# Spreading PEER gates to a table per expert: one fp32 product per token, or two products in the rounded 32-bit form

## The chip, the cores and the metric

The kernel runs on one core of a Trainium2 chip. The metric is the device time of one execution in microseconds (us). Engines are named as in the profile: PE is TensorE's matmuls, PEld its weight loads, DVE VectorE, ACT ScalarE, POOL GpSimd, SP SyncE, which starts most transfers.

## What is computed

One block of a network on x (1024 tokens x 1024): a gated recurrence and an attention in parallel, an output projection, then PEER, a retrieval over 128 x 128 single-neuron experts, and a last norm. The change is in PEER:

```python
q = (hf @ w_q).reshape(t, 8, 2, 128)
sc = einsum('thpc,hpnc->thpn', q, subkeys)
s1, i1 = top_k(sc[:, :, 0], 16); s2, i2 = top_k(sc[:, :, 1], 16)
top_s, top_p = top_k(pairs of s1 + s2, 16)
e1, e2 = the two numbers (0..127) of each chosen expert     # 8 heads x 16 = 128 per token
gates = softmax(top_s).reshape(t, 128)
pre = einsum('td,tkd->tk', h, u_tab[e1 * 128 + e2])
y = einsum('tk,tkd->td', gelu(pre) * gates, v_tab[e1 * 128 + e2])
```

## The kernel before, in words

The first three tiles of 128 tokens ("row tiles") fetch the rows of their chosen experts one by one. The other five (640 tokens) are dense: `pre` is computed for all 16384 experts and multiplied by a table of gates that is zero where an expert wasn't chosen. This table, for each token a 128 x 128 matrix over first and second number, is what the change makes in another way.

`experts_up` does this stage. Its outer loop runs over 128 blocks c of 128 experts, each cut into four quarters q (512 in all), and every engine has its own list of work by quarter. In a block:

- SP loads the next 512 KB of the turned u table (`wq_then_u`, two buffers), and stores the block's activations.
- ACT rounds it (`high`, L1637, written as `wq_then_uT_hi`); DVE (or POOL for blocks below 42 and the last four) subtracts for the rest (`low`, L1804 or L1706).
- PE multiplies (L1603): 48 products of 320 columns per block, 24 for each half of the tokens, in the rounded 32-bit form (float32r), of which one product is one pass. ACT takes the gelu of each half (L1651).
- POOL fetches rows for the row tiles by indirect DMA (L1717) into a ring of seven, and DVE multiplies and sums them (`dot`, L1737), about four per block.
- From quarter 136 on, DVE turns the choices of a dense tile into numbers (`key`, seven steps, L1240, L1244, L1246, one step every four quarters, so over some seven blocks), PE transposes them and DVE keeps them (`keep`).
- From quarter 166 to 500, 160 groups g of four tokens are spread, about two per block. For group g, which PE spreads at quarter Q: DVE writes a one-hot of the first number at Q-5 (`hot_group`, L1814); ACT writes |n - second| at Q-5 (`distance`, L1661) and relu(gate - gate * |n - second|), that is the gate where n is the second number and else 0, at Q-4 (`gate`, L1669); PE multiplies the two, per token a 128 x 128 x 128 product in fp32 (`spread_out`, L1591), and ACT copies the group out at Q (L1644). SP stores eight groups at a time (2 MB).

An engine works its list in order, so a wait holds all that stands behind it. ACT's list of a quarter is: `high`, `gelu`, `spread_out`, `distance`, `gate`. DVE's is: `low`, `key`, `keep`, `hot_group`, dots. `high(c+1)` stands at the first quarter of block c and `low(c+1)` at the second, so both may lag about four quarters behind PE before PE waits. `experts_down` (L2098) follows; the change doesn't touch it.

Of the kernel before, what the change touches and what calls it, by code (L numbers as in the profile page):

```python
# [4 lines left out]
ALU = mybir.AluOpType  # L5
# [8 lines left out]
P = 128  # L14
# [1432 lines left out]
def experts_up(nc, d, m, sem):  # L1447
# [12 lines left out]
    GROUP, SLOTS, PART = 4, 4, 8  # L1460
    GROUPS = P // GROUP
# [36 lines left out]
    with ExitStack() as own_memory:  # L1498
# [5 lines left out]
        first_hot = sb("first_hot", [P, SLOTS, GROUP, NK])  # L1504
        second = sb("gated_second_hot", [P, SLOTS, GROUP, NK])
# [7 lines left out]
        minus = sb("minus_second_and_gate", [P, 2, 2, P])  # L1513
# [13 lines left out]
        hot_done, apart_done, gates_hot = sem("hot_done"), sem("second_apart"), sem("gates_hot")  # L1527
# [9 lines left out]
        each = lambda values: values.rearrange("p (t a) -> p t a", a=1).to_broadcast([P, GROUP, NK])  # L1537

# [7 lines left out]
        with nc.Block() as block:  # L1546
# [37 lines left out]
            def _(pe):  # L1584
                def spread_out(g):
                    pe.wait_ge(hot_done, g + 1)
                    pe.wait_ge(gates_hot, g + 1)
                    if g >= 2:
                        pe.wait_ge(spread_read, g - 1)
                    for j in range(GROUP):  # L1590
                        last = nc.tensor.matmul(spread_ps[:, g % 2, j], first_hot[:, g % SLOTS, j],  # L1591
                                                second[:, g % SLOTS, j], start=True, stop=True)
                    last.then_inc(spread_done, 1)
# [14 lines left out]
                def turn_route(t):  # L1608
                    pe.wait_ge(key_step, KEY_STEPS * (nth[t] + 1))
                    if dense_nth[t]:  # L1610
                        pe.wait_ge(routeT_done, 2 * dense_nth[t])
# [18 lines left out]
            def _(act):  # L1630
# [23 lines left out]
                def distance(g):  # L1654
                    i, first = g // GROUPS, g % GROUPS * GROUP
                    if first == 0:
                        act.wait_ge(routeT_done, 2 * i + 2)
                    if g >= SLOTS:
                        act.wait_ge(spread_done, g - SLOTS + 1)
                    for j in range(GROUP):  # L1660
                        last = A(second[:, g % SLOTS, j], m.iota[:], ACT.Abs,  # L1661
                                 bias=minus[:, i % 2, 0, first + j:first + j + 1])
                    last.then_inc(apart_done, 1)

                def gate(g):
                    i, first = g // GROUPS, g % GROUPS * GROUP
                    act.wait_ge(apart_done, g + 1)
                    for j in range(GROUP):
                        last = A(second[:, g % SLOTS, j], second[:, g % SLOTS, j], ACT.Relu,  # L1669
                                 scale=minus[:, i % 2, 1, first + j:first + j + 1],  # L1670
                                 bias=routeT[:, i % 2, 2, first + j:first + j + 1])
                    last.then_inc(gates_hot, 1)

                for q in range(QUARTERS):
# [15 lines left out]
                    for g in hots_at(q):  # L1690
                        distance(g)
# [36 lines left out]
            def _(dve):  # L1728
# [3 lines left out]
                v.tensor_copy(places[:], m.iota[:, 0:TOP])  # L1732

# [56 lines left out]
                def keep(t, n):  # L1790
                    i = dense_nth[t]
                    if n == 0:
# [3 lines left out]
                        v.tensor_copy(routeT[:, i % 2], route_ps[:]).then_inc(routeT_done, 1)  # L1796
                    else:
                        dve.wait_ge(routeT_done, 2 * i + 1)
                        v.tensor_scalar(minus[:, i % 2], routeT[:, i % 2, 1:3], -1.0, None, ALU.mult
                                        ).then_inc(routeT_done, 1)  # L1800
# [6 lines left out]
                def hot_group(g):  # L1807
                    i, first = g // GROUPS, g % GROUPS * GROUP
                    tokens = slice(first, first + GROUP)
                    if first == 0:  # L1810
                        dve.wait_ge(routeT_done, 2 * i + 1)
                    if g >= SLOTS:
                        dve.wait_ge(spread_done, g - SLOTS + 1)
                    v.tensor_tensor(first_hot[:, g % SLOTS], keys, each(routeT[:, i % 2, 0, tokens]), ALU.is_equal  # L1814
                                    ).then_inc(hot_done, 1)

                for q in range(KEYS_FROM, QUARTERS + 4):
# [8 lines left out]
                    for n in range(2):  # L1826
                        for t in tiles_at(q, TURN_AFTER + 2 + n):
# [474 lines left out]
```

## Time and profile before

| | |
|---|---|
| median of 3 runs | 2829.38 us (2820.77 to 2845.56) |
| profiled execution, its span | 2830.1 us |
| PE, PEld busy | 2707.8 us (96%), 2374.9 us (84%) |
| DVE, ACT, POOL busy | 2303.6 (81%), 1251.7 (44%), 1441.5 us (51%) |
| transfers | 762.66 MB, mean 269 GB/s over the span |
| gates are spread | 1151 to 1893 us |

A busy share is the union of an engine's instructions over the span. Ends of matmuls are modelled, so for PE the distance from one start to the next tells more than a duration. On ACT and DVE too an instruction begins before the recorded end of the one in front, so what it adds is the distance between starts. "Idle before, releaser" names what ended a wait.

### The profile page before, as it was taken

The page shows a single profiled execution, that of the slowest core. Times are in us where ns is not written, and L with a number is a line of the kernel's source. Part 1 is how long each engine was busy: PE and PEld are TensorE (multiplying, and loading weights), DVE is VectorE, ACT ScalarE, POOL GpSimd, SP SyncE. Part 2 cuts the span into 40 slices and gives each one's busy share as a digit, 9 for nine tenths or more (in the row PEclk, how much of TensorE's full clock was granted, in tenths as well). Part 3 has the DMA queues.
Part 4 walks back from the last instruction along what each step waited for, and adds up shares of the span by engine and source line. Part 5 has one row for each costly group of instructions (what it writes and reads, how often), then busy time and mean ns, then how long its engine had stood idle before and what let it go on. Part 6 is the DMA issues. An engine that isn't in the chain of part 4 may idle for free. (4 is left out here: it accounts for less than half of the span.)

```text
span 2830.1 us, 39999 instructions
## 1 busy us (share of the span) xinstructions
PE 2707.8 (96%) x14923; PEld 2374.9 (84%) x14923; DVE 2303.6 (81%) x4084; ACT 1251.7 (44%) x2540; POOL 1441.5 (51%) x932
## 2 busy tenths in 40 slices
PE   7999799989999999999999999989999999999998
PEld 6777566449999999999999999987778888878877
DVE  3293896238989999797989797776999999999997
ACT  4244443113332222798888888873222222222222
POOL 1011321004328885666767566662666656656562
PEclk9999899989999999999999999999999999999999
DMA  4110100223228886999999999999999999999995
GB/s 119 42 38 23 60 1 13 85 75 101 71 62 309 302 296 218 336 368 387 382 398 393 380 391 394 390 390 337 374 369 383 385 387 388 386 389 372 391 378 216
DMA packets 332114, 762.66 MB, mean 269 GB/s; under 512 B 23232, under 2 KB 158400, under 8 KB 329360
## 3 DMA queue, kind: packets, MB, share of 16 engines
q0 software_dynamic: 111104, 403.02, 37.9%
q1 hardware_dynamic: 220096, 353.67, 35.2%
q10 hardware_dynamic: 720, 3.41, 0.3%
q8 instruction: 118, 1.93, 0.3%
q14 instruction: 76, 0.62, 0.1%
HBM read 667.73 MB, written 92.27 MB: 269 GB/s over the span
## 5 line engine op out<-in xcount | busy, mean ns | idle before, releaser
L1968 POOL DMA_INDIRECT v_rows<-in_peer_v,row_numbers x336 | 525.0, 1562 | 347.6 <-DVE y_rest L2041 202.1
L1603 PE MATMUL expert_pre<-h2T,wq_then_uT_hi 128*128 128x320 f32 x4096 | 674.7, 314 | 22.7 <-ACT wq_then_uT_hi L1637 20.3
L1717 POOL DMA_INDIRECT u_rows<-in_peer_u,row_numbers x384 | 554.1, 1443 | 243.5 <-DVE row_weights L1737 154.7
L1603 PEld LDWEIGHTS expert_pre<-h2T,wq_then_uT_hi 128*128 128x128 f32 x4096 | 613.9, 190 | 25.0 <-issue 24.9
L2098 PE MATMUL expert_out<-v_hi,w_hi 128*128 128x512 f32 x1280 | 501.9, 392 | 17.7 <-DVE w_lo L2019 16.7
L1737 DVE CUSTOM_DVE_ANT_0 u_rows<-u_rows,h_rows_kept 128x1024 f32<-128x1024 f32 x384 | 491.9, 1310 | 23.7 <-DMA u_rows<-in_peer_u,row_numbers 23.5
L2098 PE MATMUL expert_out<-v_lo,w_hi 128*128 128x512 f32 x1280 | 500.1, 391 | 0.0
L2098 PE MATMUL expert_out<-v_hi,w_lo 128*128 128x512 f32 x1280 | 500.0, 391 | 0.0
L2041 DVE SCALAR_TENSOR_TENSOR y_rest<-v_rows,row_weights,y_rest 128x1024 f32<-128x1024 f32 x256 | 327.4, 1283 | 25.9 <-DMA v_rows<-in_peer_v,row_numbers 25.5
L1603 PE MATMUL expert_pre<-h2T,wq_then_uT_lo 128*128 128x320 f32 x2048 | 343.2, 310 | 0.2 <-POOL wq_then_uT_lo L1706 0.2
L1603 PEld LDWEIGHTS expert_pre<-h2T,wq_then_uT_lo 128*128 128x128 f32 x2048 | 311.8, 188 | 0.6 <-POOL wq_then_uT_lo L1706 0.5
L1988 ACT ACTIVATE w_hi<-pick_memory 128x640 fp32r<-128x640 f32 x128 | 94.7, 740 | 481.0 <-DVE pick_memory L2012 470.8
L2098 PEld LDWEIGHTS expert_out<-v_hi,w_hi 128*128 128x128 f32 x1280 | 241.6, 189 | 72.8 <-DVE w_lo L2019 21.2
L2098 PEld LDWEIGHTS expert_out<-v_hi,w_lo 128*128 128x128 f32 x1280 | 241.4, 189 | 50.4
L2098 PEld LDWEIGHTS expert_out<-v_lo,w_hi 128*128 128x128 f32 x1280 | 241.6, 189 | 49.6
L1669 ACT ACTIVATE gated_second_hot<-gated_second_hot,routeT,minus_second_and_gate 128x128 f32<-128x128 f32 x640 | 265.8, 503 | 0.2
L1986 ACT ACTIVATE v_hi<-pick_memory 128x1024 fp32r<-128x1024 f32 x128 | 134.8, 1053 | 161.0 <-PE expert_out L2098 80.1
L1661 ACT ACTIVATE gated_second_hot<-iota,minus_second_and_gate 128x128 f32<-128x128 f32 x640 | 205.9, 409 | 0.0
L1651 ACT ACTIVATE expert_acts<-expert_pre 128x320 f32<-128x320 f32 x256 | 111.5, 436 | 212.3 <-PE expert_pre L1603 180.9
L1637 ACT ACTIVATE wq_then_uT_hi<-wq_then_u 128x1024 fp32r<-128x1024 f32 x127 | 134.8, 1062 | 125.9 <-DMA wq_then_u<-in_peer_u_turned 124.2
L1309 POOL TENSOR_TENSOR wq_then_uT_lo<-wq_then_u,wq_then_uT_hi 128x1024 fp32r<-128x1024 f32 x30 | 72.4, 2412 | 223.2 <-ACT wq_then_uT_hi L1404 223.2
L1804 DVE TENSOR_TENSOR wq_then_uT_lo<-wq_then_u,wq_then_uT_hi 128x1024 fp32r<-128x1024 f32 x82 | 100.5, 1225 | 102.9 <-ACT wq_then_uT_hi L1637 93.4
(326 smaller groups left out, 4171.1 us busy)
## 6 DMA issues: line engine op xcount, KB each, us to landing
wq_then_u<-in_peer_u_turned SPq DMA_DIRECT2D x128, 512.0 KB
pick_memory<-in_peer_v SPq DMA_DIRECT2D x128, 512.0 KB
pick_memory<-acts_dram SPq DMA_DIRECT2D x128, 320.0 KB
acts_dram<-expert_acts SPq DMA_DIRECT2D x124, 320.0 KB
pick_memory<-gates_dram SPq DMA_DIRECT2D x31, 1280.0 KB
gates_dram<-pick_memory SPq DMA_DIRECT2D x19, 2048.0 KB
wq_then_u<-in_peer_wq SPq DMA_DIRECT2D x32, 512.0 KB, 3.9
w_in_columns<-in_w_in SPq DMA_DIRECT2D x20, 512.0 KB, 4.0
```

The source lines that it names most:

```text
L1603: last = nc.tensor.matmul(pre[:, (2 * c + half) % 4, 0:WIDTH], part[:, c % 2, k], m.h2T[:, t, k, HALVES[half]], start=n == 0, stop=n == le ...
L1637: A(uhi[:, c % 2], u[c % U_RING], ACT.Copy).then_inc(uhi_done, 1)
L1651: A(act_out[:, c % 2, half * WIDTH:(half + 1) * WIDTH], pre[:, (2 * c + half) % 4, 0:WIDTH], ACT.Gelu_apprx_tanh).then_inc(act_done, 1)
L1661: last = A(second[:, g % SLOTS, j], m.iota[:], ACT.Abs, bias=minus[:, i % 2, 0, first + j:first + j + 1])
L1669: last = A(second[:, g % SLOTS, j], second[:, g % SLOTS, j], ACT.Relu, scale=minus[:, i % 2, 1, first + j:first + j + 1], bias=routeT[:, i ...
L1717: pool.indirect_dma_start(rows[:, k % RING], None, table, bass.IndirectOffsetOnAxis(ap=m.row_of[:, f, slot:slot + 1], axis=0)).then_inc(fe ...
L1737: v.tensor_tensor_reduce(out=rows[:, k % RING], in0=rows[:, k % RING], in1=m.h2_kept[:, f], scale=1.0, scalar=0.0, op0=ALU.mult, op1=ALU.a ...
L1804: v.tensor_tensor(ulo[:, c % 2], u[c % U_RING], uhi[:, c % 2].bitcast(F32), ALU.subtract).then_inc(ulo_dve, 1)
L1968: pool.indirect_dma_start(rows[:, k % ROW_RING], None, d.peer_v, bass.IndirectOffsetOnAxis(ap=m.row_of[:, f, slot:slot + 1], axis=0)).then ...
L1986: nc.scalar.activation(vhi[:, n % 2, c], vt[x % V_RING], ACT.Copy).then_inc(vhi_done, 1)
L2041: v.scalar_tensor_tensor(out=m.y_of(f), in0=rows[:, k % ROW_RING], scalar=m.row_weight[:, f, slot:slot + 1], in1=m.y_of(f), op0=ALU.mult, ...
L2098: last = nc.tensor.matmul(out[:, bank], a[:, n % 2, c, tokens], e[:, n % 2, c, cols], start=opens and c == 0 and k == 0, stop=closes and c ...
```

## The change

Per token there are now two products in float32r that add up in PSUM, one with the gate's rounded part and one with the rest; both have the first number's one-hot as weights. DVE writes the second one-hot as well, in bf16, for four tokens in one instruction with the token innermost, and ACT multiplies it by the two parts of the gate.

```diff
-        first_hot = sb("first_hot", [P, SLOTS, GROUP, NK])
-        second = sb("gated_second_hot", [P, SLOTS, GROUP, NK])
+        first_hot = sb("first_hot", [P, SLOTS, GROUP, NK], F32R)
+        second_hot = sb("second_hot", [P, HOTS, NK, GROUP], BF16)          # HOTS = 2
+        gated = sb("gated_second_hi_lo", [P, GATED, 2, GROUP, NK], F32R)   # GATED = 3
+        each_key = sb("each_key", [P, NK, GROUP], BF16)
@@ PE, spread_out
                     for j in range(GROUP):
-                        last = nc.tensor.matmul(spread_ps[:, g % 2, j], first_hot[:, g % SLOTS, j],
-                                                second[:, g % SLOTS, j], start=True, stop=True)
+                        for half in range(2):
+                            last = nc.tensor.matmul(spread_ps[:, g % 2, j], first_hot[:, g % SLOTS, j],
+                                                    gated[:, g % GATED, half, j], start=half == 0, stop=half == 1)
@@ ACT: distance(g) and its place at Q-5 are gone
                 def gate(g):
...
+                    if g >= GATED:
+                        act.wait_ge(spread_done, g - GATED + 1)
+                    act.wait_ge(second_done, g + 1)
                     for j in range(GROUP):
-                        last = A(second[:, g % SLOTS, j], second[:, g % SLOTS, j], ACT.Relu,
-                                 scale=minus[:, i % 2, 1, first + j:first + j + 1],
-                                 bias=routeT[:, i % 2, 2, first + j:first + j + 1])
+                        for half, part in enumerate((gate_hi.bitcast(F32), gate_lo)):
+                            last = A(gated[:, g % GATED, half, j], second_hot[:, g % HOTS, :, j], ACT.Copy,
+                                     scale=part[:, i % 2, first + j:first + j + 1])
@@ DVE, keep: four steps per tile instead of two
+                    elif n == 1:
+                        dve.wait_ge(routeT_done, KEEP_STEPS * i + 1)
+                        made = v.tensor_copy(second_of[:, i % 2], routeT[:, i % 2, 1])
+                    elif n == 2:
+                        made = v.tensor_copy(gate_hi[:, i % 2], routeT[:, i % 2, 2])
                     else:
-                        v.tensor_scalar(minus[:, i % 2], routeT[:, i % 2, 1:3], -1.0, None, ALU.mult
+                        made = v.tensor_tensor(gate_lo[:, i % 2], routeT[:, i % 2, 2], gate_hi[:, i % 2].bitcast(F32),
+                                               ALU.subtract)
@@ DVE, hot_group
+                    if g >= HOTS:
+                        dve.wait_ge(gates_hot, g - HOTS + 1)
+                    v.tensor_tensor(second_hot[:, g % HOTS], each_key[:], over_keys(second_of[:, i % 2, tokens]),
+                                    ALU.is_equal).then_inc(second_done, 1)
```

PE at the first group, before and after. `wq_then_uT_hi` and `_lo` are the u table's two parts, `expert_pre` the block's products:

```order
L1603 MATMUL expert_pre<-h2T,wq_then_uT_hi 128x320 x12
L1591 MATMUL spread_ps<-gated_second_hot,first_hot 128x128 x4
L1603 MATMUL expert_pre<-h2T,wq_then_uT_hi 128x320 x4
L1603 MATMUL expert_pre<-h2T,wq_then_uT_lo 128x320 x8
L1603 MATMUL expert_pre<-h2T,wq_then_uT_hi 128x320 x12
L1591 MATMUL spread_ps<-gated_second_hot,first_hot 128x128 x4
```

```order
L1609 MATMUL expert_pre<-h2T,wq_then_uT_hi 128x320 x12
L1597 MATMUL spread_ps<-gated_second_hi_lo,first_hot 128x128 x8
L1609 MATMUL expert_pre<-h2T,wq_then_uT_hi 128x320 x4
L1609 MATMUL expert_pre<-h2T,wq_then_uT_lo 128x320 x8
L1609 MATMUL expert_pre<-h2T,wq_then_uT_hi 128x320 x12
L1597 MATMUL spread_ps<-gated_second_hi_lo,first_hot 128x128 x8
```

Eight products stand where four stood, each with 128 columns. The place among the large products is the same.

ACT at the start of block 79's rounding, before and after (`pick_memory` holds the spread groups on their way out):

```order
L1651 ACTIVATE expert_acts<-expert_pre 128x320
L1661 ACTIVATE gated_second_hot<-iota,minus_second_and_gate 128x128 x4
L1637 ACTIVATE wq_then_uT_hi<-wq_then_u 128x1024
L1644 ACTIVATE pick_memory<-spread_ps 128x128x4
L1669 ACTIVATE gated_second_hot<-gated_second_hot,routeT,minus_second_and_gate 128x128 x4
L1651 ACTIVATE expert_acts<-expert_pre 128x320
L1661 ACTIVATE gated_second_hot<-iota,minus_second_and_gate 128x128 x4
```

```order
L1669 ACTIVATE gated_second_hi_lo<-second_hot,gate_lo 128x128
L1657 ACTIVATE expert_acts<-expert_pre 128x320
L1643 ACTIVATE wq_then_uT_hi<-wq_then_u 128x1024
L1650 ACTIVATE pick_memory<-spread_ps 128x128x4
L1669 ACTIVATE gated_second_hi_lo<-second_hot,gate_hi 128x128
L1669 ACTIVATE gated_second_hi_lo<-second_hot,gate_lo 128x128
L1669 ACTIVATE gated_second_hi_lo<-second_hot,gate_hi 128x128
```

The four `distance` instructions behind the gelu are gone, and `gate` has eight instructions (hi and lo in turn) for four.

DVE at the first key step of a dense tile, before and after:

```order
L1240 TENSOR_TENSOR pick_memory<-pair_digits,places 128x2048
L1737 ISA u_rows,row_weights<-u_rows,h_rows_kept 128x1024
L1737 ISA row_weights 128x1
L1804 TENSOR_TENSOR wq_then_uT_lo<-wq_then_u,wq_then_uT_hi 128x1024
L1814 TENSOR_TENSOR first_hot<-iota,routeT 128x512
L1737 ISA u_rows,row_weights<-u_rows,h_rows_kept 128x1024
L1737 ISA row_weights 128x1
L1737 ISA u_rows,row_weights<-u_rows,h_rows_kept 128x1024
```

```order
L1240 TENSOR_TENSOR pick_memory<-pair_digits,places 128x2048
L1735 ISA u_rows,row_weights<-u_rows,h_rows_kept 128x1024
L1735 ISA row_weights 128x1
L1808 TENSOR_TENSOR wq_then_uT_lo<-wq_then_u,wq_then_uT_hi 128x1024
L1818 TENSOR_TENSOR first_hot<-iota,routeT 128x512
L1822 TENSOR_TENSOR second_hot<-each_key,second_numbers 128x512
L1735 ISA u_rows,row_weights<-u_rows,h_rows_kept 128x1024
L1735 ISA row_weights 128x1
L1735 ISA u_rows,row_weights<-u_rows,h_rows_kept 128x1024
```

Behind every `first_hot` there is now a `second_hot`; the dots and `low` stand behind it.

## Rows read from the trace of the kernel before

**Rows 1.** Stage window (start:end, length; busy us per engine; PEclk, DMA share, GB/s)
```profile
1151.00:1893.00 742.00, 731.54 (x5265) 728.57 (x5264) 629.16 (x907) 641.55 (x1673) 493.75 (x336) 1.00 1.00 385
```

**Rows 2.** Groups by line, 1151 to 1893 us: count | busy us, mean ns | idle before
```profile
L1603 PE MATMUL expert_pre<-h2T,wq_then_uT_hi 128*128 128x320 f32 x2647 | 443.7, 315 | 10.2 <-ACT wq_then_uT_hi L1637 10.2
L1669 ACT ACTIVATE gated_second_hot<-gated_second_hot,routeT,minus_second_and_gate 128x128 f32<-128x128 f32 x632 | 262.5, 504 | 0.2
L1603 PE MATMUL expert_pre<-h2T,wq_then_uT_lo 128*128 128x320 f32 x1328 | 221.9, 309 | 0.2 <-POOL wq_then_uT_lo L1706 0.2
L1661 ACT ACTIVATE gated_second_hot<-iota,minus_second_and_gate 128x128 f32<-128x128 f32 x630 | 202.8, 409 | 0.0
L1591 PE MATMUL spread_ps<-gated_second_hot,first_hot 128*128 128x128 f32 x1278 | 168.4, 275 | 0.0
```

**Rows 3.** Waits, same stretch: waiting line, releaser, us in total, times, longest
```profile
ACT wq_then_uT_hi L1637 <- DMA wq_then_u<-in_peer_u_turned: 92.6, 21, 6.3
DVE wq_then_uT_lo L1804 <- ACT wq_then_uT_hi L1637: 86.4, 44, 7.2
DVE u_rows L1737 <- DMA u_rows<-in_peer_u,row_numbers: 15.0, 11, 3.4
```

**Rows 4.** Timeline of TensorE, one half block: start, length, instructions merged
```profile
1499.88 1.05 PE L1591 MATMUL spread_ps<-gated_second_hot,first_hot 128*128 128x128 f32 x8
1502.53 1.93 PE L1603 MATMUL expert_pre<-h2T,wq_then_uT_hi 128*128 128x320 f32 x12
1504.29 1.05 PE L1591 MATMUL spread_ps<-gated_second_hot,first_hot 128*128 128x128 f32 x8
```

**Rows 5.** Timeline of TensorE in attention, rounded 32-bit products, starts 128 columns
```profile
451.67 0.28 PE L704 MATMUL logits<-later_keys,unit 128*128 128x128 f32 x1
451.79 0.33 PE L699 MATMUL logits<-k_hi_twice,q_hi_and_lo 128*128 128x256 f32 x1
452.08 0.22 PE L704 MATMUL logits<-later_keys,unit 128*128 128x128 f32 x1
452.14 0.39 PE L699 MATMUL logits<-k_hi_twice,q_hi_and_lo 128*128 128x384 f32 x1
```

**Rows 6.** Lines L1240 and L1244 (bf16): duration ns min/median/max
```profile
L1240 DVE TENSOR_TENSOR pick_memory<-pair_digits,places x10: 2283/2290/2294, 1106.8 to 1664.2; 128x2048 bf16<-128x2048 bf16 x10
L1244 DVE TENSOR_TENSOR pick_memory<-pick_memory,top_indices_f x10: 1222/1227/3316, 1109.1 to 1673.3; 128x2048 bf16<-128x2048 bf16 x10
```

**Rows 7.** Windows of eight blocks, without key steps first, then with
```profile
1255.40:1326.00 70.60, 69.54 (x502) 69.06 (x501) 54.89 (x88) 59.60 (x159) 45.77 (x33) 1.00 1.00 389
1326.00:1396.60 70.60, 67.94 (x489) 67.32 (x488) 64.40 (x92) 59.90 (x158) 48.85 (x32) 1.00 0.99 379
1467.20:1537.80 70.60, 70.55 (x510) 70.10 (x509) 67.50 (x98) 64.41 (x170) 51.72 (x34) 1.00 1.00 390
```

**Rows 8.** Timeline of ScalarE behind a late load, and the group TensorE spreads next
```profile
1505.95 1.06 ACT L1637 ACTIVATE wq_then_uT_hi<-wq_then_u 128x1024 fp32r<-128x1024 f32 x1 [5.40 <-DMA wq_then_u<-in_peer_u_turned]
1507.39 1.64 ACT L1669 ACTIVATE gated_second_hot<-gated_second_hot,routeT,minus_second_and_gate 128x128 f32<-128x128 f32 x4
1508.93 0.42 ACT L1651 ACTIVATE expert_acts<-expert_pre 128x320 f32<-128x320 f32 x1
1509.25 1.27 ACT L1661 ACTIVATE gated_second_hot<-iota,minus_second_and_gate 128x128 f32<-128x128 f32 x4
1510.42 0.58 ACT L1644 ACTIVATE pick_memory<-spread_ps 128x512 f32<-128x512 f32 x1
1509.13 1.13 PE L1591 MATMUL spread_ps<-gated_second_hot,first_hot 128*128 128x128 f32 x8
```

**Rows 9.** Timeline in a key stretch: a first one-hot, and its group on TensorE
```profile
1368.23 0.69 DVE L1814 TENSOR_TENSOR first_hot<-iota,routeT 128x512 f32<-128x512 f32 x1
1368.83 1.22 DVE L1737 CUSTOM_DVE_ANT_0 u_rows<-u_rows,h_rows_kept 128x1024 f32<-128x1024 f32 x1
1370.06 1.05 PE L1591 MATMUL spread_ps<-gated_second_hot,first_hot 128*128 128x128 f32 x8
```

More of the change, by code:

```diff
@@ L1460, in experts_up @@
     GROUP, SLOTS, PART = 4, 4, 8
+    HOTS, GATED, KEEP_STEPS = 2, 3, 4
     GROUPS = P // GROUP
@@ L1652, in gelu, with gate @@
                       ACT.Gelu_apprx_tanh).then_inc(act_done, 1)
-                def distance(g):
+                def gate(g):
                     i, first = g // GROUPS, g % GROUPS * GROUP
                     if first == 0:
-                        act.wait_ge(routeT_done, 2 * i + 2)
-                    if g >= SLOTS:
-                        act.wait_ge(spread_done, g - SLOTS + 1)
+                        act.wait_ge(routeT_done, KEEP_STEPS * (i + 1))
+                    if g >= GATED:
+                        act.wait_ge(spread_done, g - GATED + 1)
+                    act.wait_ge(second_done, g + 1)
                     for j in range(GROUP):
[L1661 to L1668, printed above, removed]
-                        last = A(second[:, g % SLOTS, j], second[:, g % SLOTS, j], ACT.Relu,
-                                 scale=minus[:, i % 2, 1, first + j:first + j + 1],
-                                 bias=routeT[:, i % 2, 2, first + j:first + j + 1])
+                        for half, part in enumerate((gate_hi.bitcast(F32), gate_lo)):
+                            last = A(gated[:, g % GATED, half, j], second_hot[:, g % HOTS, :, j], ACT.Copy,
+                                     scale=part[:, i % 2, first + j:first + j + 1])
                     last.then_inc(gates_hot, 1)
@@ L1689, in _ @@
                                           ).then_inc(spread_stored[g // PART % 2], 16)
-                    for g in hots_at(q):
-                        distance(g)
                     for g in gates_at(q):
@@ L1732, in _ @@
                 v.tensor_copy(places[:], m.iota[:, 0:TOP])
+                v.tensor_copy(each_key[:], m.iota[:].rearrange("p (n a) -> p n a", a=1).to_broadcast([P, NK, GROUP]))
                 def dot(k):
@@ L1825, in _ @@
                             key(t, n)
-                    for n in range(2):
-                        for t in tiles_at(q, TURN_AFTER + 2 + n):
+                    for n in range(KEEP_STEPS):
+                        for t in tiles_at(q, TURN_AFTER + 2 + n // 2):
                             if t >= F:
```

16 lines of the change are left out of this document (9 added, 7 removed).

## The prediction

> **What bounds the kernel now.** I first looked at the stretch in which gates are spread, 742 us of the span [rows 1]. There PE is busy for 732 us, the granted clock is 1.00 (2.4 GHz), the transfer engines are at 1.00 with 385 GB/s, ACT is busy for 642 us and DVE for 629 us. PE and transfers are both nearly full, so it has to be asked which one waits for the other.
>
> The groups by line tell how many blocks that is: 2647 + 1328 large products [rows 2] at 48 a block are 82.8 blocks, 8.96 us each. The timeline gives PE's own price: twelve large products take 1504.29 - 1502.53 = 1.76 us, 147 ns each, and from one group's start to the next, with 24 large products between, 4.41 us pass [rows 4]. So a group of four tokens costs 4.41 - 24 x 0.147 = 0.88 us, and eight records at 111 ns give the same. A block with two groups is 48 x 0.147 + 2 x 0.88 = 8.82 us; the 160 groups are 1.92 a block, so PE needs 8.75 us of the 8.96. About 17 us in the stretch are PE's waits, 10 of them for ACT's rounding of the u table [rows 2].
>
> Those come from transfers. ACT waits 21 times, 92.6 us in all, for a u table block, and DVE waits 86.4 us for ACT behind it [rows 3]. PE only feels it when the four quarters by which ACT may lag are used up. So: PE bound, with transfers a close second, and ACT and DVE in step with both.
>
> **PE: eight one-pass products for four fp32 ones.** In the trace an fp32 product already shows as two products and two weight loads (1278 records for 640 products, [rows 2]); now there are two products with one load each, so eight pairs a group as before. The question is what a pair costs. In attention there are float32r products of 128 columns. Where a wide product stands in front, which hides the weight load, the next product starts 60 ns later (452.08 to 452.14). Where narrow ones follow one another, it starts 120 ns later (451.67 to 451.79) [rows 5]. A pair alone is therefore set by its weight load, some 110 to 120 ns, not by its pass. The spread products are just such a row of narrow ones, and the second product of a token loads the same one-hot again, since each product of the program brings its load (as many loads as products in every line of the trace). So 8 x 111 to 8 x 120 ns: 0.89 to 0.96 us for 0.88, that is 0 to +12 us in 160 groups. I take 0, since the fp32 pairs with the same 128-column loads stand at 111. The bound from below is 8 x 60 = 0.48 us, rival 1.
>
> **ACT.** Before, the four instructions of `gate` take 1508.93 - 1507.39 = 1.54 us between starts (385 ns each, scale and bias per partition), the four of `distance` 1510.42 - 1509.25 = 1.17 us (293 ns each, one pointer) [rows 8]. The new ones have one pointer, so 8 x 293 = 2.34 us for 2.71: 60 us less in all. If reading bf16 with a step of four made each as dear as 385 ns, it would be 3.08 us, 59 us more. I take 293, by the number of pointers. ACT isn't the bound, but it catches up behind late loads, so part of it may count: at most the 17 us of PE's waits. The other side is that `gate` behind a late load takes 0.80 us longer (2.34 for 1.54), and there PE stands behind it: ACT's `gate` ends at 1507.39 + 1.64 = 1509.03, PE spreads at 1509.13 [rows 8]. With a group at about every second quarter, some 10 of 21 late loads are hit: +8 us. For the quicker catching up I take off 9 us, half of the 17.
>
> **DVE: the second one-hot.** 160 instructions over 512 bf16 elements. Both bounds are in the trace: with a broadcast operand along the innermost axis 2048 bf16 elements take 2290 ns (L1240), with the innermost axis contiguous in all operands 1227 ns (L1244) [rows 6]. The new one is of the second kind (token innermost, read with step one from both). `first_hot` takes 0.60 us between starts for 512 elements in 32 bits [rows 9], and an element 1063 / 1024 = 1.04 ns, so with half the steps it is 0.60 - 256 x 0.00104 = 0.33 us. It is a comparison as in L1240, and a multiplication in L1244, which leaves the doubt; I take 0.33, the row with the same layout, and 0.60 as the upper end. [...] So +53 us (up to +96) of DVE work, which had 113 us of idle time in the stretch [rows 1]. Two more small steps per dense tile are under 2 us.
>
> Where does it hurt? In eight blocks without key steps DVE is busy 54.9 us, with them 64.4 to 67.5 [rows 7], 8.05 to 8.44 us a block; 1.92 x 0.33 = 0.63 more make 8.7 to 9.1 against PE's 8.82. So in the key stretches of four tiles DVE is as full as PE. And there is a new wait: ACT's `gate` now waits for the second one-hot, and behind it in ACT's list are gelu, `high` and the copies out. Before, PE alone needed the one-hot, five quarters later. In a key stretch the lead was used up: a first one-hot ends at 1368.92 and its group starts on PE at 1370.06, 1.14 us later [rows 9]. Now 0.33 us and ACT's 2.34 + 0.12 us must fit in, 1.65 us too much. Two such places in each of four stretches would be +13 us; in the stretch of 1467 to 1538 us PE had no idle time [rows 7], so I count half, +7 us.
>
> **Sum.** 0 + 8 - 9 + 7 = +6 us on the profiled 2830.1, so 2836. That execution is 0.7 us above the median of 2829.4, which I leave aside. Nothing before 1107 us (the first key step) or behind the stretch is touched, and no byte moves that didn't before.
>
> **Rival 1, PE gets quicker.** If the loads hide behind the passes, a group falls from 0.88 towards 0.48 us, 65 us of PE in all. But then transfers bind: at 390 instead of 385 GB/s [rows 1, 7] the same bytes take 732 us, 10 us less, and ACT and DVE are held by the same loads; with the finer waits gone perhaps 20. Time 2810 to 2820. For it: the pass alone is 60 ns. Against it: the 120 ns between narrow ones [rows 5]. The Trainium skill (TensorE: Matmul & The Clock Gate, "Back-to-back issue gap") states about 81 ns for pairs of load and product at 128 columns; by it a group would be 0.65 us and PE would save 37 us, with the same end at the transfers. The trace's 111 and 120 ns speak against it. Chance 14%, of which 5% go beyond 1%.
>
> **Rival 2, the hand-over binds.** If the second one-hot takes 0.60 us, key stretches need 8.25 + 1.15 = 9.4 us a block on DVE, 0.6 us over PE's 8.82: some 33 blocks, +19 us. DVE's 15 us of waits for rows [rows 3] then also reach ACT through `gate`, and PE, since the lead is gone: +15. With the 6 above, 2870. It decides from 0.33 us for the one-hot, since (8.82 - 8.2) / 1.92 = 0.32. ACT at 385 ns a piece would do the same: 1.92 x 0.37 = 0.7 us on its 7.7 leaves ACT at 8.4 of 8.82, which a wait for DVE turns into the bound. Chance 18%, of which 14% above 1%.
>
> **Numbers.** What this kernel's measurement tells from no change I take as 1%, 28 us. The main case has 68%: 2822 to 2855, from the bounds of ACT's relief and of PE's pairs. Faster by over 1% 0.05, within 0.80, slower 0.15. The range takes in most of both rivals: 2812 to 2866.
>
> **What would show it.** Starts of the new products 110 to 120 ns apart, and a block with two groups still at 8.8 us: the PE step; at 60 to 80 ns, rival 1. The second one-hot at about 0.42 us recorded against 0.69: the DVE step. ACT's waits for a second one-hot in the key stretches, and PE waiting behind `gate`; if they sum to over 20 us, rival 2. ACT's copies at 409 ns recorded, not 504. I am wrong in kind if transfers change, or if PE waits outside the stretch.

## The result, and the profile after

| | us |
|---|---|
| before, median of 20 runs | 2829.27 (2820.71 to 2845.56) |
| after, median of 20 runs | 2838.18 (2832.76 to 2846.50) |
| ratio after to before | 1.0030, 95% interval 1.0019 to 1.0041 |
| predicted | 2836, range 2812 to 2866 |

The change costs 9 us, 0.3%: 5 to 12 us by the interval. That is less than the 1% that I had called no change, and with this many runs it is still told from zero. The profiled execution took 2833.5 us, with a span of 2831.7, so it is one of the quicker ones of after. In it the last block's work of the up stage ends at 1937 us, for 1926 us before, and the down stage, which the change doesn't touch, happened to be 9 us shorter. So the stage windows have to be compared, not the spans.

Windows of after: the stretch of [rows 1], the key stretch of [rows 7], and 28 us inside that, to which I come back. Columns as in [rows 1]:

```profile
1151.00:1893.00 742.00, 727.70 (x5203) 722.93 (x5203) 672.07 (x1067) 596.10 (x1658) 502.86 (x330) 0.99 0.99 381
1326.00:1396.60 70.60, 67.51 (x485) 66.54 (x483) 68.73 (x105) 52.53 (x148) 51.07 (x33) 1.00 0.97 373
1384.00:1412.00 28.00, 23.72 (x147) 22.88 (x146) 24.62 (x42) 20.58 (x61) 17.81 (x12) 0.88 0.96 370
```

Over the same 742 us DVE went from 629 to 672 us, ACT from 642 to 596, PE from 732 to 728. PE did less in the stretch because the stage advances more slowly. In the key stretch DVE is at 68.73 of 70.60 us, for 64.40.

The groups of after in that stretch, next to [rows 2] and [rows 9]:

```profile
L1669 ACT ACTIVATE gated_second_hi_lo<-second_hot,gate_hi 128x128 fp32r<-128x128 bf16 x626 | 254.3, 406 | 44.0 <-DVE second_hot L1822 43.6
...
L1597 PE MATMUL spread_ps<-gated_second_hi_lo,first_hot 128*128 128x128 f32 x1256 | 159.1, 270 | 6.3 <-issue 5.9 <-DVE first_hot L1818 0.4
...
L1818 DVE TENSOR_TENSOR first_hot<-iota,routeT 128x512 fp32r<-128x512 f32 x157 | 107.1, 682 | 0.0
...
L1822 DVE TENSOR_TENSOR second_hot<-each_key,second_numbers 128x512 bf16<-128x512 bf16 x157 | 65.1, 415 | 0.0
```

Each sort of instruction costs nearly what its row had promised. ACT's copies take 406 ns recorded, where I had expected 409, and the second one-hot 415 ns, where I had expected about 420. From start to start a copy takes 302 ns, which is 2.42 us a group for 2.71 before.

TensorE's timeline, one half block of after, the place of [rows 4]:

```profile
1500.21 1.00 PE L1597 MATMUL spread_ps<-gated_second_hi_lo,first_hot 128*128 128x128 f32 x8
...
1502.86 1.92 PE L1609 MATMUL expert_pre<-h2T,wq_then_uT_hi 128*128 128x320 f32 x12
1504.62 1.00 PE L1597 MATMUL spread_ps<-gated_second_hi_lo,first_hot 128*128 128x128 f32 x8
```

From one group's start to the next pass 1504.62 - 1500.21 = 4.41 us, to the hundredth what it was before. Twice that is 8.82 us a block, so PE's own price did not move.

The waits in the stretch, next to [rows 3]; the third is new:

```profile
ACT wq_then_uT_hi L1643 <- DMA wq_then_u<-in_peer_u_turned: 83.1, 28, 6.5
...
DVE wq_then_uT_lo L1808 <- ACT wq_then_uT_hi L1643: 54.3, 23, 5.5
ACT gated_second_hi_lo L1669 <- DVE second_hot L1822: 43.6, 32, 3.7
...
PE expert_pre L1609 <- ACT wq_then_uT_hi L1643: 7.3, 6, 3.4
```

So PE costs the same, ACT works 45 us less, DVE 43 us more, and ACT waits 44 us for the second one-hot. PE itself shows only 7 us of waits for ACT, and yet the stage is longer. How that comes about can be read from SP's list. SP stores the activations of a block as soon as its second gelu is done, and *behind that*, in the same order, it starts the next load of the u table. In the stretch of after, SP waited 82 times for the gelu before a store, 654 us in all, and no wait for anything else stands before a load: the gelu decides when a load starts. The starts of the stores, before and then after, in the same key stretch (start, length, queue, what moves):

```profile
1367.73 0.32 SPq L1558 DMA_DIRECT2D acts_dram<-expert_acts  x1
...
1375.71 0.32 SPq L1558 DMA_DIRECT2D acts_dram<-expert_acts  x1
...
1383.69 0.32 SPq L1558 DMA_DIRECT2D acts_dram<-expert_acts  x1
```

```profile
1364.09 0.32 SPq L1563 DMA_DIRECT2D acts_dram<-expert_acts  x1
...
1373.88 0.32 SPq L1563 DMA_DIRECT2D acts_dram<-expert_acts  x1
...
1382.63 0.32 SPq L1563 DMA_DIRECT2D acts_dram<-expert_acts  x1
...
1392.40 0.32 SPq L1563 DMA_DIRECT2D acts_dram<-expert_acts  x1
1392.76 0.43 SPq L1557 DMA_DIRECT2D wq_then_u<-in_peer_u_turned  x1
```

Before, they stand 7.98 us apart. That is not PE's pace (8.82 us a block): it is ACT, running flat out, catching up on a load that came late, 0.84 us a block. In the whole stage 59 of the 83 distances between stores are under 8.5 us, and 19, one every four or five blocks, are 10.7 to 14.4 us, where a load is late again. After, in this key stretch, they are 9.79, 8.75 and 9.77 us: ACT doesn't catch up but falls further behind, and each load of the u table goes out later with its store (1392.76, right behind the store at 1392.40).

How one of these places runs (timeline of after; in brackets the idle time before and its releaser):

```profile
1371.02 0.41 ACT L1669 ACTIVATE gated_second_hi_lo<-second_hot,gate_hi 128x128 fp32r<-128x128 bf16 x1 [2.30 <-DVE second_hot L1822]
...
1382.99 0.43 SPq L1569 DMA_DIRECT2D gates_dram<-pick_memory  x1
...
1383.47 0.51 SPq L1557 DMA_DIRECT2D wq_then_u<-in_peer_u_turned  x1
...
1386.23 2.27 DVE L1246 TENSOR_REDUCE route<-pick_memory 128x128 f32<-128x2048 bf16 x1
...
1389.03 0.41 DVE L1822 TENSOR_TENSOR second_hot<-each_key,second_numbers 128x512 bf16<-128x512 bf16 x1
...
1389.53 0.42 ACT L1669 ACTIVATE gated_second_hi_lo<-second_hot,gate_hi 128x128 fp32r<-128x128 bf16 x1 [2.30 <-DVE second_hot L1822]
...
1391.96 0.41 ACT L1657 ACTIVATE expert_acts<-expert_pre 128x320 f32<-128x320 f32 x1
...
1393.71 1.33 PE L1609 MATMUL expert_pre<-h2T,wq_then_uT_lo 128*128 128x320 f32 x8
...
1397.25 1.06 ACT L1643 ACTIVATE wq_then_uT_hi<-wq_then_u 128x1024 fp32r<-128x1024 f32 x1 [4.87 <-DMA wq_then_u<-in_peer_u_turned]
...
1398.45 2.62 PE L1609 MATMUL expert_pre<-h2T,wq_then_uT_hi 128*128 128x320 f32 x12 [3.40 <-ACT wq_then_uT_hi L1643]
...
1401.30 1.94 PE L1597 MATMUL spread_ps<-gated_second_hi_lo,first_hot 128*128 128x128 f32 x8 [0.24 <-issue]
...
1404.22 2.32 PE L1609 MATMUL expert_pre<-h2T,wq_then_uT_lo 128*128 128x320 f32 x8
```

A key step of 2.27 us (L1246) stands ahead of the one-hots on DVE. ACT's gate waits 2.30 us for the second one-hot, the gelu comes at 1391.96 for that reason, and with it the store at 1392.40 and the load at 1392.76. This load does no harm: it landed 9.1 us later, before ACT asked for its block at 1404.66. The harm comes from the same kind of wait in the blocks before. ACT had waited 3.74 us at 1361.22, 2.30 at 1371.02 and 1.23 at 1379.74, each time for a second one-hot, and so the load of the block that ACT rounds at 1397.25 started at 1383.47, where before it had started at 1376.56, 6.91 us earlier. It took 13.8 us to land. ACT therefore rounds that block 6.06 us later than in before (1397.25 for 1391.19), and PE has waited 3.40 us for it, for 1.86.

Why is it this load that is late, and not the one behind it? Right ahead of it, at 1382.99, SP had started a store of eight groups (2 MB). In the stretch of after, the 19 loads that start right behind such a store landed 12.3 to 14.9 us after their start, and all others 5.7 to 11.8 us after it. Before has the same pattern: 19 of ACT's 21 waits for the u table [rows 3], with 92.2 of the 92.6 us, end 12.4 to 15.1 us after such a store has started. So the late loads that the prediction took from the rows as given come with the stores of the spread groups, one every four or five blocks. No run moved or split these stores, so what they cost isn't measured.

Then comes something that I had not counted at all: the products behind the wait take longer. Eight large products take 2.32 us instead of 1.33, and eight narrow ones 1.94 instead of 1.0. The granted clock from 1399.60 to 1406.40 is 0.50, the lower level of 1.2 GHz; over the 28 us it is 0.88.

### The profile page after: what moved, and what is told of

Read it like the earlier page. It is cut to its first block and busy times, and to the rows that moved or that the text cites. A ratio compares the mean times of both kernels' runs of the same rounds, so it can differ in the third digit from the quotient of the medians.

```text
span 2831.7 us, 40324 instructions
## 1 busy us (share of the span) xinstructions
PE 2710.0 (96%) x14923; PEld 2374.3 (84%) x14923; DVE 2360.4 (83%) x4255; ACT 1212.3 (43%) x2540; POOL 1454.3 (51%) x932
## 5 line engine op out<-in xcount | busy, mean ns | idle before, releaser
L1714 POOL DMA_INDIRECT u_rows<-in_peer_u,row_numbers x384 | 570.1, 1485 | 234.2 <-DVE row_weights L1735 142.7
L1669 ACT ACTIVATE gated_second_hi_lo<-second_hot,gate_hi 128x128 fp32r<-128x128 bf16 x640 | 259.9, 406 | 45.8 <-DVE second_hot L1822 45.3
L1669 ACT ACTIVATE gated_second_hi_lo<-second_hot,gate_lo 128x128 fp32r<-128x128 bf16 x640 | 259.3, 405 | 0.0
L2033 DVE TENSOR_TENSOR v_lo<-pick_memory,v_hi 128x1024 fp32r<-128x1024 f32 x128 | 155.7, 1217 | 20.1 <-ACT v_hi L1994 20.1
```

The source lines that it names most:

```text
L1669: last = A(gated[:, g % GATED, half, j], second_hot[:, g % HOTS, :, j], ACT.Copy, scale=part[:, i % 2, first + j:first + j + 1])
L1714: pool.indirect_dma_start(rows[:, k % RING], None, table, bass.IndirectOffsetOnAxis(ap=m.row_of[:, f, slot:slot + 1], axis=0)).then_inc(fe ...
L2033: v.tensor_tensor(vlo[:, n % 2, c], vt[x % V_RING], vhi[:, n % 2, c].bitcast(F32), ALU.subtract).then_inc(vlo_done, 1)
```

## The experiments

Twelve kernels; the ratios are to the kernel before, with 95% intervals, run on the same chip. 1% is 28 us.

**e1: TensorE's part alone.** The kernel before, with one-hots in float32r and the product issued twice.

```diff
-        first_hot = sb("first_hot", [P, SLOTS, GROUP, NK])
+        first_hot = sb("first_hot", [P, SLOTS, GROUP, NK], F32R)
-                        last = nc.tensor.matmul(spread_ps[:, g % 2, j], ..., start=True, stop=True)
+                        for half in range(2):
+                            last = nc.tensor.matmul(spread_ps[:, g % 2, j], ..., start=half == 0, stop=half == 1)
```

> The kernel before with one part of the change alone: one-hot and gated one-hot are written as float32r, and each token's product is issued twice, as two one-pass products with the same operands (the gates come out doubled and rounded; ACT's, DVE's and all other work is as before). My theory: a pair of weight load and product stays at 111 ns, a block with two groups at 8.82 us, time within 4 us of before (ratio 0.999 to 1.0015). Rival 1 (the loads hide and a pair costs 60 to 80 ns): blocks of 7.9 to 8.3 us, 10 to 20 us faster (0.993 to 0.9965).

Measured: 0.9999 (0.9988 to 1.0010). The window and one group of its timeline:

```profile
1151.00:1893.00 742.00, 731.35 (x5253) 728.56 (x5252) 627.75 (x908) 641.22 (x1675) 489.22 (x334) 1.00 1.00 385
```

```profile
1501.27 1.00 PE L1592 MATMUL spread_ps<-gated_second_hot,first_hot 128*128 128x128 f32 x8
```

The window is that of before, and from this group's start to the next (1505.69) it is 4.42 us. Two float32r products cost what one fp32 product does. Rival 1, the quicker PE, is refuted, and, to within 3 us, what the change does to the time comes from the way the one-hots are made.

**e2: the second one-hot two quarters earlier,** with a third buffer.

```diff
-    HOTS, GATED, KEEP_STEPS = 2, 3, 4
+    HOTS, GATED, KEEP_STEPS = 3, 3, 4
+                    for g in groups_at(q + 7):
+                        second_group(g)       # second_hot, moved out of hot_group, which stands at q + 5
```

> The change with the second one-hot written seven quarters before its product in place of five, and three buffers for it in place of two; nothing else moves. My theory (the hand-over DVE to ACT in key stretches is what costs): ACT's 44 us of waits for the second one-hot fall under 10 us, and the ratio to before falls from 1.003 to 0.999 to 1.001. If the cost were DVE's added work itself (it is as full as PE in key stretches), ACT's waits turn into PE's waits for the low part of the u table or for its rounding, and the ratio stays at 1.002 to 1.004.

Measured: 0.9945 (0.9925 to 0.9965). Its wait for the second one-hot, and its windows of [rows 7]:

```profile
ACT gated_second_hi_lo L1669 <- DVE second_hot L1828: 1.3, 2, 0.8
```

```profile
1326.00:1396.60 70.60, 70.60 (x511) 70.42 (x509) 70.60 (x109) 58.69 (x165) 49.45 (x31) 1.00 1.00 390
1467.20:1537.80 70.60, 70.59 (x510) 70.33 (x510) 70.60 (x109) 59.81 (x167) 51.29 (x33) 1.00 1.01 392
```

The 43.6 us of waits are 1.3. Against the change itself that is 0.9945 / 1.0030 = 0.9916, 24 us faster (17 to 30, both intervals taken together). So the short lead costs about 24 us, not the 7 that I had booked. And since this kernel is 16 us *faster* than before, which no theory had expected, the change must contain a larger gain than the 9 us that I had counted. The windows also show DVE at 70.60 of 70.60 us, exactly full, while PE is full as well. (The execution profiled took 2827.4 us, one of the two longest of e2's six, whose median is 2817.7.)

**e9: the third buffer alone,** since e2 had changed two things.

```diff
-    HOTS, GATED, KEEP_STEPS = 2, 3, 4
+    HOTS, GATED, KEEP_STEPS = 3, 3, 4
```

> The change with three buffers for the second one-hot instead of two, its place left where the change has it (beside the first one-hot, one quarter ahead of ScalarE's gate). e2 moved the instruction two quarters earlier and added this third buffer at once; this run tells the two apart. My theory (what costs is the short lead between the one-hot and gate): a third buffer alone gives nothing, 1.002 to 1.004 of the kernel before like the change, and ScalarE's waits for the second one-hot stay at 35 to 50 us in the stretch from 1151 to 1893 us. Rival (with two buffers VectorE is held by ScalarE's gate of two groups ago, and that holds its dots and the low parts): the third buffer takes most of e2's gain by itself, 0.995 to 0.997.

Measured: 1.0029 (1.0017 to 1.0041), the change's own ratio.

```profile
ACT gated_second_hi_lo L1669 <- DVE second_hot L1822: 44.6, 32, 3.7
```

The waits stay too. It is the lead, not the buffer.

**e3: the second one-hot made dearer.** Second numbers kept in 32 bits, so that the comparison reads one operand in bf16 and one in fp32.

```diff
-        second_of = sb("second_numbers", [P, 2, P], BF16)
+        second_of = sb("second_numbers", [P, 2, P])
```

> The change with the second numbers kept in 32 bits, so that the comparison reads one bf16 and one 32-bit operand; same output, same places. It raises one cost. Expected: the second one-hot goes from 415 to about 690 ns (0.60 us between starts in place of 0.335), 42 us more of DVE work. My theory, by rival 2's price of the prediction: DVE then needs over 9.2 us a block in key stretches, and the kernel is 20 to 40 us slower than before (1.007 to 1.014). If DVE has room and only the place of the hand-over counts, 10 to 15 us (1.0035 to 1.0055).

Measured: 1.0056 (1.0039 to 1.0073). The instruction (ns min/median/max) and ACT's wait for it:

```profile
L1822 DVE TENSOR_TENSOR second_hot<-each_key,second_numbers x160: 675/684/3292, 1141.8 to 1912.9; 128x512 bf16<-128x512 bf16 x160
```

```profile
ACT gated_second_hi_lo L1669 <- DVE second_hot L1822: 77.8, 59, 4.0
```

The instruction went from 415 to 684 ns, 43 us of work in all, and ACT's waits from 43.6 to 77.8 us. Against the change it costs only 0.26%, 7 us (2 to 13). Rival 2, which saw DVE at the point where any more time binds at once, had called for 1.007 or more.

**e10: the same dearer one-hot, but with e2's lead.** Edit: e2 and e3 together.

> e2 (second one-hot two quarters earlier, three buffers) with the second numbers kept in 32 bits, so that the one-hot takes about 0.27 us longer, as in e3: 43 us more VectorE work, with the lead in place. My theory (VectorE's load costs only through the hand-over): what e3 paid for it (0.26%) mostly goes away or stays as small, so 0.9945 to 0.998 of the kernel before, and ScalarE's waits for the second one-hot stay under 10 us. Rival (VectorE is the bound in the key stretches whatever the lead, some 33 blocks): the 43 us of work over 160 groups cost 0.5 us in each of these blocks, 16 us, so 1.000 to 1.001.

Measured: 1.0003 (0.9993 to 1.0013). Windows and waits:

```profile
1326.00:1396.60 70.60, 69.39 (x497) 68.38 (x495) 70.25 (x100) 56.93 (x160) 42.13 (x29) 1.00 0.98 379
1467.20:1537.80 70.60, 68.62 (x490) 67.63 (x489) 68.29 (x101) 56.38 (x156) 44.28 (x30) 1.00 0.99 376
```

```profile
ACT gated_second_hi_lo L1669 <- DVE second_hot L1828: 10.0, 11, 2.6
PE expert_pre L1609 <- DVE wq_then_uT_lo L1808: 8.4, 9, 2.3
```

My expectation was wrong here, and the rival's number came. With the lead in place the same 43 us of DVE work cost 0.58%, 16 us (10 to 23). Next to e2 the two windows show why: there DVE was full to the hundredth, and here PE falls from 70.6 to 69.39 and 68.62 us and waits for DVE's `low`. In e3 the same work cost 7 us (2 to 13), which may be less because ACT, held by the hand-over, already kept everything back; that is my reading, and the two intervals overlap. So DVE's load does count once the key stretches are full, and in e2 they are.

**e11: the second one-hot's work on the kernel before, read by nobody.**

```diff
+                    v.tensor_tensor(spare_hot[:, g % 2], each_key[:], ...spare_number[:, i % 2, tokens]..., ALU.is_equal)
```

> The kernel before with one added instruction a group on VectorE: the second one-hot's form (128x512, bf16, is_equal), right behind the first one-hot, over numbers that nothing depends on, and read by nobody. So it is VectorE's 53 us of added work alone, with no hand-over. e10 showed 43 us of VectorE work to cost 16 us when it comes on top of e2. Theory A (VectorE is at its edge only after the second one-hot is there; e2's key stretches have it busy 70.60 of 70.60 us): the first 53 us cost little, 1.000 to 1.002 of the kernel before. Theory B (each us of VectorE work costs the same 0.37 us): 53 us cost 20 us, 1.006 to 1.008; ScalarE's relief would then be worth more than e7's 13 us, some 36 us.

Measured: 0.9984 (0.9972 to 0.9996). DVE is busy for 681 us of the stretch, for 629, and ACT for 643, for 642.

The first 53 us of DVE's work are free, as theory A had it, though the time came out below its range. That they should even gain 4 us I can't explain: the fetches of rows are started by POOL when DVE has finished with a row, so later dots move transfers, but I didn't test it.

**e12: ACT's relief alone.** Before, with one of the four `distance` instructions of a group left out (`gate` is edited to read another token's; not shown).

```diff
-                    for j in range(GROUP):
+                    for j in range(GROUP - 1):
                         last = A(second[:, g % SLOTS, j], m.iota[:], ACT.Abs,
```

> The kernel before with one of ScalarE's four distance instructions of a group left out (the fourth token's gate reads the first token's distance, so its one-hot is another's): 0.29 us less a group, 47 us in all, about what the change takes off ScalarE (2.71 to 2.42 us), with no work added to VectorE and no new hand-over. If ScalarE's relief is worth what e7 took back (0.47%): 0.995 to 0.996 of the kernel before. Under theory B of the run before it would be 0.987 to 0.990. If ScalarE's relief is worth nothing by itself, because the transfers bind: 0.999 to 1.001.

Measured: 0.9916 (0.9902 to 0.9930), 24 us faster (20 to 28) for 47 us less work. The window, PE's group, and SP's stores:

```profile
1151.00:1893.00 742.00, 739.24 (x5344) 738.18 (x5342) 640.76 (x916) 606.54 (x1526) 490.86 (x340) 1.00 1.00 393
```

```profile
L1603 PE MATMUL expert_pre<-h2T,wq_then_uT_hi 128*128 128x320 f32 x2700 | 450.3, 314 | 1.8 <-ACT wq_then_uT_hi L1637 1.8
```

```profile
1340.56 0.32 SPq L1558 DMA_DIRECT2D acts_dram<-expert_acts  x1
...
1347.95 0.32 SPq L1558 DMA_DIRECT2D acts_dram<-expert_acts  x1
...
1358.77 0.32 SPq L1558 DMA_DIRECT2D acts_dram<-expert_acts  x1
...
1366.17 0.32 SPq L1558 DMA_DIRECT2D acts_dram<-expert_acts  x1
```

PE's waits for ACT in this group fell from 10.2 us to 1.8, and the stage advances by 2700 of these products for 2647. The stores stand 7.39 and 7.40 us apart where ACT catches up (the 10.82 between them is a late load): 1.42 us a block under PE's 8.82 instead of 0.84. This is the gain inside the change. It is larger than what I had expected from e7 (0.995 to 0.996) and smaller than theory B's.

**e7: ACT's relief taken back.** e2 with a ninth copy per group, read by nobody.

```diff
+                    A(spare[:, g % GATED], second_hot[:, g % HOTS, :, 0], ACT.Copy, scale=gate_lo[...])
```

> The change with the earlier second one-hot, and a ninth copy per group on ACT whose result nobody reads: ACT's gate costs 2.64 us a group in place of 2.34 (before: 2.72 with the distances). Nothing else moves. Theory (the 0.5% below before in that run came from ACT's 60 us of relief): most of it goes, ratio 0.998 to 1.001. Rival (it came from elsewhere, the split between engines or a later start of transfers): stays at 0.993 to 0.997.

Measured: 0.9992 (0.9980 to 1.0005). Against e2, 47 us of ACT work cost 0.47%, 13 us (6 to 20). Together with e12: a microsecond of ACT work is worth 0.3 us of time here and 0.5 us there, though ACT was busy for only 86% of the stretch of before.

e7 also says what it costs that all of ACT's work stands in `gate`. It and e11 have the same work on ACT (2.72 and 2.71 us a group) and on DVE; in e11 the `gate` has 1.54 us of it, in e7 all. Between the two lie +2 us (-3 to +7).

**e4: the product with the low part left out.**

```diff
-                        for half in range(2):
-                            last = nc.tensor.matmul(spread_ps[:, g % 2, j], ..., gated[:, g % GATED, half, j], ...
+                        last = nc.tensor.matmul(spread_ps[:, g % 2, j], ..., gated[:, g % GATED, 0, j], ...
```

> The change with the product of the gate's low part left out (one product per token, gates rounded; ACT still writes both parts). It takes 640 pairs off PE. If a pair costs 111 ns and PE bounds the stage alone, 71 us go. My theory: transfers are a close second (share 1.00, 385 GB/s), and ACT and DVE are in step with them, so a block falls from 8.83 to 8.6 us at best and 5 to 20 us go (ratio to before 0.995 to 1.001). If PE were the bound alone: 0.977 to 0.985.

Measured: 1.0006 (0.9992 to 1.0020). Its waits:

```profile
ACT wq_then_uT_hi L1642 <- DMA wq_then_u<-in_peer_u_turned: 95.6, 32, 8.6
...
PE expert_pre L1608 <- ACT wq_then_uT_hi L1642: 51.7, 20, 5.7
```

640 pairs of 111 ns are 71 us less for PE, and 7 us (2 to 12) come out. PE's wait for ACT went from 7.3 to 51.7 us: the freed time becomes waiting, behind ACT and the loads. Another part of it goes to the clock, which behind these waits was granted at 0.97 over the stretch, for 0.99 in the change: PE's busy time fell by 50 us only (727.7 to 677.3). With the hand-over as it is, PE isn't what paces the stage.

**e5 and e6: one copy per token.** The second one-hot by DVE as in the change, but one ACT copy with the whole gate and one fp32 product; `gate_hi` and `gate_lo` are gone. e6 has e2's lead in addition.

```diff
-                        for half, part in enumerate((gate_hi.bitcast(F32), gate_lo)):
-                            last = A(gated[:, g % GATED, half, j], second_hot[:, g % HOTS, :, j], ACT.Copy,
-                                     scale=part[:, i % 2, first + j:first + j + 1])
+                        last = A(gated[:, g % GATED, j], second_hot[:, g % HOTS, :, j], ACT.Copy,
+                                 scale=routeT[:, i % 2, 2, first + j:first + j + 1])
```

> The change with the fp32 product kept: the second one-hot comes from DVE in bf16 at the same place, ACT multiplies it by the whole gate in one copy per token (four for eight per group), PE does one fp32 product per token; same output as before. PE unchanged at 8.83 us a block, DVE as in the change, ACT 1.2 us a group in place of 2.4 (and 2.7 before). Theory (ACT's relief pays, the hand-over costs): the hand-over's cost of the change is there, but behind a late load or a late one-hot the gate takes half as long, so the ratio to before is 0.992 to 0.998. Rival (transfers and DVE alone set the rest): 1.000 to 1.003, as the change.

> The same with the second one-hot two quarters earlier and three buffers. Theory: both gains add up as far as transfers allow, ratio 0.987 to 0.994. Rival: the earlier one-hot already took all that is to be had, ratio 0.993 to 0.996, as that run (0.9945).

Measured: e5 0.9928 (0.9906 to 0.9950), e6 0.9913 (0.9893 to 0.9934). e5's wait for the one-hot; then e6's window, and ACT's wait for PE's spread product in it:

```profile
ACT gated_second L1666 <- DVE second_hot L1813: 109.2, 76, 4.4
```

```profile
1151.00:1893.00 742.00, 740.50 (x5355) 739.73 (x5354) 691.25 (x1075) 433.90 (x1054) 519.66 (x342) 1.00 1.00 393
```

```profile
ACT pick_memory L1648 <- PE spread_ps L1595: 105.1, 106, 2.5
```

e5 waits longest of all for the second one-hot, 109 us, and is fast all the same: with four copies a group ACT (430 us busy) has the time to wait. The two don't differ by more than their intervals. In e6 PE is busy 740.50 of 742 us and ACT waits for PE. At 2808.93 us, 23 us less than its own chip's 2832.11, it has the shortest median of the versions that keep the gate whole.

**e8: e6 with one float32r product,** the gate rounded to that form.

> The version with one copy per token and the earlier one-hot, with the product in float32r: one pass and one weight load per token in place of an fp32 product's two (the gate is rounded; nothing else moves). It takes 640 pairs of 111 ns, 71 us, off PE where neither the hand-over nor ACT stands in the way. Theory 1 (PE bounds that version: its stage of 730.7 us for 83 blocks is 8.80 us each, PE's own price): it gets faster, but transfers, at a share of 1.00 and 393 GB/s, stop it early: 0 to 15 us beyond the 0.9913, ratio 0.986 to 0.992. Theory 2 (PE bounds alone): 0.966 to 0.972.

Measured: 0.9874 (0.9847 to 0.9900), 2797.29 us. Window and ACT's wait for the u table:

```profile
1151.00:1893.00 742.00, 697.78 (x4795) 687.29 (x4793) 696.81 (x1075) 432.37 (x1055) 516.69 (x342) 0.99 1.01 400
```

```profile
ACT wq_then_uT_hi L1641 <- DMA wq_then_u<-in_peer_u_turned: 148.8, 48, 8.6
```

Half of the products are gone, 71 us of PE, and 0.39% comes out against e6, 11 us (1 to 21). ACT's waits for loads rise from 96 to 149 us and the traffic to 400 GB/s. Once PE is relieved the transfers bind, as the prediction had it for rival 1, but not they alone: PE's longest waits are now for DVE's `low` (31.2 us; 8.7 for ACT's `high`), and from 1326 to 1396.6 us DVE is busy for 70.60 of 70.60 us and PE for 64.53. This run doesn't separate the two.

## Why the prediction was right, and where its terms were not

**PE, 0 us: right.** Starts 111 ns apart, a block at 8.82 us, and e1 at -0.3 us (-3 to +3). The Trainium skill (TensorE: Matmul & The Clock Gate, "Back-to-back issue gap") would have put a pair at about 81 ns. No run here shows that; every row of narrow products, in either form, has its starts 111 ns apart, but for the first step of a row in after (60 ns).

**The second one-hot, 0.33 us, and ACT's copies, 293 ns: right.** They measure 0.335 us and 302 ns from start to start, so ACT is relieved by 46 us where I had counted 60.

**ACT's relief, -9 us: too small.** e12 gives -24 us for about the same 47 us of work, and e7 against e2 gives 13 us (6 to 20). The step that failed is the cap: "at most the 17 us of PE's waits". The waits in which PE stands for ACT by name are only the end of a chain. ACT also decides when SP's store goes, and behind it the next load, so a faster ACT moves the transfers too. The number that should have been looked at is the distance between the stores before: 7.98 us, not 8.82. It says that for most of the stage ACT ran flat out. e12 bears this out: with 2 x 0.29 us less work a block the distance is 7.40.

**The hand-over, +7 us: too small.** e2 against the change gives 24 us, and e9 shows that it is the lead. I had counted two places in each of four key stretches at 1.65 us, and halved that. The trace has 32 waits, 43.6 us in all, the longest 3.7 us; some 34 us of them fall in the four key stretches, about one wait to a key step. The price of one was computed from a single first one-hot at its usual place, while DVE's whole key steps, 2.27 us long, also stand in the way. And where PE "had no idle time" I took half off, though a late ACT comes back through the load.

**`gate` behind a late load, +8 us: not found.** e7 against e11 gives +2 us (-3 to +7) for it.

**The parts don't simply add up.** By e11 (-4) and e12 (-24) e2 would be at -28 us. It is at -16 (-21 to -10), some 12 us short. With e7 the gap has a place: ACT's relief is worth 24 us where DVE has room (e12), and 13 us where the second one-hot's work is on DVE too (e7 to e2). Why a fuller DVE takes away from it is open: in e2 DVE is full in the key stretches, but no run isolates that. The gap itself is known only to some 8 us.

**The sum.** Along before, e11, e7, e2 and the change the steps are -4 for DVE's work, +2 for the place of ACT's work, -13 for its relief and +24 for the hand-over. They add up to +9 because each starts where the last one ended; that is no check of its own. My terms were 0, +8, -9 and +7. My +6 had the sign, the size and the named mechanisms right, but it came out that close by luck: the hand-over was 17 us too small, and the other terms together, 14 us too dear, made up for it. For e2 or e12, where the hand-over's cost is absent, the same terms miss by some 15 us.

**Rival 2** had the right place, the key stretches, with DVE full and the lead gone, and too high a price at 0.33 us for the one-hot. By my own sign (waits of ACT that sum to over 20 us) the 43.6 us spoke for it, but the 2870 us that went with it did not come; the sign didn't tell it from the main case. That DVE's work binds beyond a point is real, though: e10 is beyond it and pays 16 us. **What would make it wrong in kind** was that transfers change. Their bytes didn't, but their starts did, in step with ACT.

## What to carry to other kernels

An engine that is busy 86% of a stage can still be what paces it: look at the distance between its periodic milestones (here the stores) and compare it with the bottleneck's own block time. If it is shorter, that engine is catching up; here it did so at full speed, and each microsecond on it counted for 0.3 to 0.5. Where a change makes one engine wait for another in the same quarter, give the producer a lead of its own before shaving its work: two quarters of lead and one small buffer were worth 24 us here. Where a load is late at a regular distance, look at what was started right ahead of it in its queue. And splitting an fp32 product into two one-pass products of 128 columns gained nothing here, as each takes 111 ns from start to start, like each of the two in which an fp32 product shows; what paid is not to need the second one, or, as in e6, to use the cheaper one-hot for fewer ACT copies.

## What the runs showed of the hardware that I had not expected

A short wait of PE in the middle of dense work can cost more than its length. Behind the 3.40 us at 1398.45 the 24 large and 8 narrow products up to 1406.35 took 7.90 us, where the same ones take 4.41 us at the full clock [rows 4]; the granted clock was 0.50 from 1399.60 to 1406.40. The length of the wait doesn't settle it. e9 waits 3.72 us at the same place and its clock is 0.51 from 1398.50 to 1401.90 (window of 28 us: 0.94). e1 waits only 1.91 us there, and its twelve large products behind the wait still take 3.45 us instead of 1.92, at 0.50. Before waits 1.86 us at 1392.39 and keeps 1.00, but behind 2.18 us at 1616.70 it falls (0.51 from 1616.60 to 1620.00); e9 keeps 1.00 behind 2.09 us at 1516.3. e4, whose PE waits 20 times and up to 5.7 us, has 0.97 over the whole stretch. These are single places, not a rule.

A comparison with one 16-bit and one 32-bit operand has lost the fast rate: 684 ns in e3 for 415 ns with both in bf16, which is `first_hot`'s 682 ns in 32 bits.

ACT reads bf16 with a step of four elements at hardly any price: 406 ns recorded, where the fp32 reads of `distance` took 409 [rows 2], and from start to start 302 ns for 293.
